# Input stage of a hybrid decoder step: the sample sequences' mLSTM state products on column tiles and row tiles of TensorE

## The reference

```python
m_t = jnp.maximum(inter, jnp.max(dlog, axis=-1))
wts = jnp.exp(dlog - m_t[..., None]) * jnp.einsum('bhtd,bhsd->bhts', q_c, k_c)
w_prev = jnp.exp(inter - m_t)
num = w_prev[..., None] * jnp.einsum('bhtd,bhde->bhte', q_c, C) + jnp.einsum('bhts,bhse->bhte', wts, v_c)
den = w_prev * jnp.einsum('bhtd,bhd->bht', q_c, n) + jnp.sum(wts, axis=-1)
h = num / jnp.maximum(jnp.abs(den), jnp.exp(-m_t))[..., None]
...
C = wp[..., None, None] * C + jnp.einsum('bhs,bhsd,bhse->bhde', ws, k_c, v_c)
```

## Time and profile before

| | |
|---|---|
| median of 3 runs | 1915.89 us (1915.38 to 1916.56) |
| profiled execution, its own time | 1918.07 us |
| its span | 1916.1 us |
| mean granted TensorE clock | 0.96 |
| DMA | 408.98 MB, mean 213 GB/s |

### The profile page before, as it was taken

How to read it: one execution, slowest core, us unless ns; L and a number is a source line. 1 busy time by engine, 2 the same in 40 slices (tenths; PEclk the granted TensorE clock), 3 DMA queues, 4 the chain that set the end, 5 groups by cost and what they waited for, 6 DMA issues and landing times. The chain is left out here.

```text
span 1916.1 us, 36779 instructions
## 1 busy us (share of the span) xinstructions
PE 1748.7 (91%) x14891; PEld 1439.4 (75%) x14891; DVE 910.2 (48%) x1610; ACT 604.8 (32%) x890; POOL 270.5 (14%) x286
## 2 busy tenths in 40 slices
PE   7999999999999999999998999999898868777675
PEld 7999899998787778778777999999796434443242
DVE  6553445555756676576665445455423222121223
ACT  5243223333443344344335333335432101110012
POOL 0550003112010100100010000850050000000002
PEclk9999999999999999999998999999998988898888
DMA  7445353434232223233215446455638999999995
GB/s 270 174 155 187 110 179 117 173 135 167 100 112 90 99 101 122 87 112 112 90 55 204 155 175 250 152 220 214 238 159 338 422 431 432 431 431 431 431 431 248
DMA packets 46600, 408.98 MB, mean 213 GB/s; under 512 B 6580, under 2 KB 8376, under 8 KB 16696
## 3 DMA queue, kind: packets, MB, share of 16 engines
q1 hardware_dynamic: 46520, 407.81, 54.2%
HBM read 396.62 MB, written 11.18 MB: 213 GB/s over the span
## 5 line engine op out<-in xcount | busy, mean ns | idle before, releaser
L387 PE MATMUL ps<-x_high,w_high 128*128 128x288 f32 x928 | 257.4, 303 | 9.3 <-ACT w_high L593 9.3
L388 PE MATMUL ps<-x_rest,w_high 128*128 128x288 f32 x928 | 253.1, 299 | 0.0
L387 PEld LDWEIGHTS ps<-x_high,w_high 128*128 128x128 f32 x928 | 177.1, 191 | 12.8 <-ACT w_high L593 10.2
L388 PEld LDWEIGHTS ps<-x_rest,w_high 128*128 128x128 f32 x928 | 177.1, 191 | 0.5
L549 ACT ACTIVATE w_high<-w_raw 128x2048 fp32r<-128x2048 f32 x57 | 109.2, 1915 | 153.9 <-DMA w_raw<-in_w_main 77.5
L1101 PE MATMUL ps<-x_high,r_high 128*128 128x288 f32 x512 | 145.8, 308 | 3.8 <-ACT r_high L1352 3.8
L660 DVE TENSOR_TENSOR w_rest<-w_raw,w_high 128x2048 fp32r<-128x2048 f32 x58 | 137.1, 2369 | 11.0 <-ACT w_high L549 11.0
L2557 PE MATMUL ps<-half_a,xg 128*32 128x512 f32 x240 | 81.4, 840 | 62.3 <-DMA half_b<-in_w_egu 62.0
L1101 PE MATMUL ps<-rx_low,r_high 128*128 128x288 f32 x480 | 134.7, 305 | 0.0
L392 PE MATMUL ps<-x_high,w_rest 128*128 128x288 f32 x928 | 132.1, 295 | 1.0 <-DVE w_rest L660 1.0
L392 PEld LDWEIGHTS ps<-x_high,w_rest 128*128 128x128 f32 x928 | 126.0, 188 | 1.2 <-DVE w_rest L660 1.2
(11 more groups left out here) (600 smaller groups left out, 3824.1 us busy)
## 6 DMA issues: line engine op xcount, KB each, us to landing
w_raw<-in_w_main SPq DMA_DIRECT2D x57, 1024.0 KB, 4.8
ring<-in_w_g SPq DMA_DIRECT2D x32, 1024.0 KB, 4.8
half_a<-in_w_egu SPq DMA_DIRECT2D x15, 2048.0 KB, 18.0
half_b<-in_w_egu SPq DMA_DIRECT2D x15, 2048.0 KB, 22.3
ring<-in_w_u SPq DMA_DIRECT2D x32, 512.0 KB, 4.2
ring<-in_w_gate SPq DMA_DIRECT2D x8, 2048.0 KB, 7.8
ring<-in_w_out SPq DMA_DIRECT2D x8, 2048.0 KB, 7.8
half_d<-in_w_egu SPq DMA_DIRECT2D x8, 2048.0 KB, 20.7
```

Of the source, the lines that this page charges most:

```text
L387: mm(o, high[:, t % 2, k, :], x_h[:, k, :], start=(k == 0), stop=False)
L388: ins = mm(o, high[:, t % 2, k, :], x_l[:, k, :], start=False, stop=False)
```

## The change

The products of the sample states run four sequences at a time. For the queries, sequence b adds to partitions 32(b mod 4) to 32(b mod 4)+32 of bank 0, a column tile of the array of its own; `cq` then has 128 rows, and the product that adds it to the numerators sums its four quadrants with a 128 x 32 constant (four identities under each other). For the keys, `decode_state` takes the rows of quadrant b mod 4, a row tile of its own, in a bank of its own (4, 5, 1, 3); all eight products stand in one group after the third group of tiles, and VectorE reads both halves of it at the places where it did. For this, the sample tokens of the values, keys and gate rows must stand on all four quadrants: each transpose of 32 columns becomes four products with the identity, one for each quadrant. `ktm` becomes 128 x 256 instead of 32 x 1024. `scores` of the next head now waits for `cB`, since banks 1 and 3 hold states.

```diff
+QUADS = P // NSM
+    c["own_seq"] = ((s % NSM) // NL == s // NSM + (P // NSM) * np.arange(NB // QUADS)[None, :])
...
-        ktm = placed("ktm", [NSM, NB, P], "ring", 14336)
+        ktm = placed("ktm", [P, NB // QUADS, P], "ring", 14336)
-        cq = placed("cq", [NSM, DV], "front", 10272)
+        cq = placed("cq", [P, DV], "front", 10272)
+        quad = lambda n: slice(NSM * n, NSM * n + NSM)
+        state_banks = (4, 5, 1, 3)
...
             def turn_values(e):
                 for c in range(3):
-                    n = P if c < 2 else NSM
                     for j in range(4):
-                        ins = nc.tensor.transpose(ps[0:n, b, j * P:(j + 1) * P], mlu[:, 8 + 4 * e + j, c * P:c * P + n], ident)
+                        o, own = ps[:, b, j * P:(j + 1) * P], mlu[:, 8 + 4 * e + j, :]
+                        if c < 2:
+                            ins = nc.tensor.transpose(o, own[:, c * P:c * P + P], ident)
+                        else:
+                            for n in range(QUADS):
+                                ins = mm(o[quad(n), :], own[:, NPR:T], ident, start=True, stop=True)
             def scores(h):
+                    pe.wait_ge(v.sem, v.at(f"cB{h - 1}"))
...
-                for c in range(3):
-                    n = P if c < 2 else NSM
-                    ins = nc.tensor.transpose(ps[0:n, 7, c * P:(c + 1) * P], kh[:, c * P:c * P + n], ident)
+                for c in range(2):
+                    nc.tensor.transpose(ps[:, 7, c * P:(c + 1) * P], kh[:, c * P:(c + 1) * P], ident)
+                for n in range(QUADS):
+                    ins = mm(ps[quad(n), 7, 2 * P:3 * P], kh[:, NPR:T], ident, start=True, stop=True)
             def numerators(h):
-                if h:
-                    pe.wait_ge(v.sem, v.at(f"cB{h - 1}"))
                 for b in range(NB):
-                    ins = mm(ps[0:NSM, 0, 0:DV], qz[:, NSM * b:NSM * b + NSM], cst[:, h % 2, b, :], start=(b == 0), stop=(b == NB - 1))
+                    ins = mm(ps[quad(b % QUADS), 0, 0:DV], qz[:, NSM * b:NSM * b + NSM], cst[:, h % 2, b, :],
+                             start=(b < QUADS), stop=(b >= NB - QUADS))
...
-                    ins = mm(ps[:, 4 + e, NPR:T], cq[:, e * P:(e + 1) * P], K("ident", NSM)[:, 0:NSM], start=False, stop=True)
+                    ins = mm(ps[:, 4 + e, NPR:T], cq[:, e * P:(e + 1) * P], K("ident_c"), start=False, stop=True)
-            def decode_state(h, part):
-                if part == "A":
-                    pe.wait_ge(g_.sem, g_.at(f"ktm{h}"))
-                    pe.wait_ge(v.sem, v.at(f"h{h}"))
-                else:
-                    pe.wait_ge(v.sem, v.at(f"cA{h}"))
-                for j in range(4):
-                    b = j + 4 * (part == "B")
-                    ins = mm(ps[:, 4 + j // 2, j % 2 * DV:(j % 2 + 1) * DV], ktm[:, b, :], vt[0:NSM, 2, h * DV:(h + 1) * DV],
+            def decode_state(h):
+                pe.wait_ge(g_.sem, g_.at(f"ktm{h}"))
+                pe.wait_ge(v.sem, v.at(f"h{h}"))
+                for b in range(NB):
+                    n, m = b % QUADS, b // QUADS
+                    ins = mm(ps[:, state_banks[n], m * DV:(m + 1) * DV], ktm[quad(n), m, :], vt[quad(n), 2, h * DV:(h + 1) * DV],
                              start=True, stop=True)
...
                 if t == GIF + 9:
-                    for c in range(3):
-                        n = P if c < 2 else NSM
-                        for i, r in enumerate((g, ws)):
-                            ins = nc.tensor.transpose(ps[0:n, 7, c * 8 + 4 * i:c * 8 + 4 * i + 4], r[:, c * P:c * P + n],
-                                                      K("ident", 4, 0, 4))
+                    for i, r in enumerate((g, ws)):
+                        for c in range(2):
+                            nc.tensor.transpose(ps[:, 7, c * 8 + 4 * i:c * 8 + 4 * i + 4], r[:, c * P:(c + 1) * P], K("ident", 4, 0, 4))
+                        for n in range(QUADS):
+                            ins = mm(ps[quad(n), 7, 16 + 4 * i:20 + 4 * i], r[:, NPR:T], K("ident", 4, 0, 4), start=True, stop=True)
...
-                decode_state(h, "A")
+                decode_state(h)
                 if h:
                     mean_square(h - 1)
                 tiles(h, 3)
-                decode_state(h, "B")
```

More of the change, by code:

```diff
@@ L270, in stage_front @@
             at_end = lambda *s: [f"{x}{h}" for x in s] if h == MLH - 1 else []
-            pe_steps += [f"{x}{h}" for x in ("s", "b", "k", "c", "n", "u", "dA")] + of_last("q") + [f"dB{h}"] + at_end("q")
+            pe_steps += [f"{x}{h}" for x in ("s", "b", "k", "c", "n", "u", "d")] + of_last("q") + at_end("q")
             dve_steps += [f"{x}{h}" for x in ("x", "qw", "qn", "w", "wm", "k", "max", "rec", "h", "n", "cA")]
@@ L471, in prompt_state @@
                 q.done(mm(ps[:, 7, DV + 1:DV + 1 + NB], kt[0:NSM, 2, :], K("of_seq", NSM), start=True, stop=True), f"u{h}")
-            def decode_state(h, part):
-                if part == "A":
-                    pe.wait_ge(g_.sem, g_.at(f"ktm{h}"))
-                    pe.wait_ge(v.sem, v.at(f"h{h}"))
-                else:
-                    pe.wait_ge(v.sem, v.at(f"cA{h}"))
-                for j in range(4):
-                    b = j + 4 * (part == "B")
-                    ins = mm(ps[:, 4 + j // 2, j % 2 * DV:(j % 2 + 1) * DV], ktm[:, b, :], vt[0:NSM, 2, h * DV:(h + 1) * DV],
+            def decode_state(h):
[4 more added lines that the diff above has]
+                    ins = mm(ps[:, state_banks[n], m * DV:(m + 1) * DV], ktm[quad(n), m, :], vt[quad(n), 2, h * DV:(h + 1) * DV],
                              start=True, stop=True)
-                q.done(ins, f"d{part}{h}")
+                q.done(ins, f"d{h}")
             def mean_square(h):
@@ L568, in values @@
                 for c in range(3):
-                    n = P if c < 2 else NSM
                     act.wait_ge(q.sem, q.at(f"vt{c}{e}"))
                     b = (0, 1, 3, 4, 5, 7)[3 * e + c]
-                    a.done(fn(vt[0:n, c, e * 512:(e + 1) * 512], ps[0:n, b, :], ACT.Copy), f"vt{c}{e}")
+                    a.done(fn(vt[:, c, e * 512:(e + 1) * 512], ps[:, b, :], ACT.Copy), f"vt{c}{e}")
             def square_of(h):
@@ L607, in _ @@
                     act.wait_ge(q.sem, q.at("gt"))
-                    fn(gt[:, 0:16], ps[:, 7, 0:16], ACT.Copy)
-                    a.done(fn(gt[0:NSM, 16:24], ps[0:NSM, 7, 16:24], ACT.Copy), "gt")
+                    a.done(fn(gt[:, 0:24], ps[:, 7, 0:24], ACT.Copy), "gt")
                 if GIF + 11 <= t < GIF + 15:
@@ L628, in _ @@
                 act.wait_ge(q.sem, q.at(f"c{h}"))
-                a.done(fn(cq[:, :], ps[0:NSM, 0, 0:DV], ACT.Copy), f"c{h}")
+                a.done(fn(cq[:, :], ps[:, 0, 0:DV], ACT.Copy), f"c{h}")
                 act.wait_ge(q.sem, q.at(f"n{h}"))
@@ L740, in weights @@
                 ts(kt[:, 1, :], ps[:, 7, P:2 * P], wsp(1), None, ALU.mult)
-                v.done(ts(kt[0:NSM, 2, :], ps[0:NSM, 7, 2 * P:3 * P], wsp(2, NSM), None, ALU.mult), f"k{h}")
+                v.done(ts(kt[:, 2, :], ps[:, 7, 2 * P:3 * P], wsp(2), None, ALU.mult), f"k{h}")
             def outcome(h):
@@ L764, in state @@
             def state(h, part):
-                dve.wait_ge(q.sem, q.at(f"d{part}{h}"))
-                for j in range(4):
-                    b = j + 4 * (part == "B")
+                dve.wait_ge(q.sem, q.at(f"d{h}"))
+                for j in range(QUADS):
+                    b = j + QUADS * (part == "B")
                     ins = stt(out=cst[:, h % 2, b, :], in0=cst[:, h % 2, b, :], scalar=wps[h % 2][:, NL * b + NL - 1:NL * b + NL],
-                              in1=ps[:, 4 + j // 2, j % 2 * DV:(j % 2 + 1) * DV], op0=ALU.mult, op1=ALU.add)
+                              in1=ps[:, state_banks[j], (b - j) // QUADS * DV:((b - j) // QUADS + 1) * DV], op0=ALU.mult, op1=ALU.add)
                 v.done(ins, f"c{part}{h}")
@@ L887, in by_sequence @@
                 if h:
-                    pool.wait_ge(q.sem, q.at(f"dB{h - 1}"))
-                g_.done(tt(ktm[:, :, :], kt[0:NSM, 2, :].unsqueeze(1).to_broadcast([NSM, NB, P]),
-                           K("of_seq", NSM).unsqueeze(2).to_broadcast([NSM, NB, P]), ALU.mult), f"ktm{h}")
+                    pool.wait_ge(q.sem, q.at(f"d{h - 1}"))
+                g_.done(tt(ktm[:, :, :], kt[:, 2, :].unsqueeze(1).to_broadcast([P, NB // QUADS, P]),
+                           K("own_seq").unsqueeze(2).to_broadcast([P, NB // QUADS, P]), ALU.mult), f"ktm{h}")
             def gated(h):
```

## The result

The median of six runs is 1904.9 us (1902.88 to 1910.31), beside 1916.22 us for the kernel before: ratio 0.9937, 95% interval [0.9923, 0.9951]. The change makes the kernel faster by 11 us; forecast were 19, and the median lies above the range of 1893.5 to 1902.5. The profiled execution has a time of 1902.88 us and a span of 1900.9.

A forecast was written before the change was run, and what follows sets the result against it. The prediction took TensorE (PE) to bound the changed stage, with the last ten slices bound by expert-weight transfers. Terms -10.1 - 10.8 + 2.1 = -18.8, rounded to -19, took the median from 1915.9 to 1897 us; range 1893.5 to 1902.5.

The forecast's parts named there:

- The query products: Changed stage: 16 passes per head on four column tiles take 1.05 us instead of 3.57, gain 10.1 us in all.
- The state products: Changed stage: one group of 1.15 us per head on four row tiles replaces two of 1.92, gain 10.8 us.
- rival 1: State products: row tiles overlap only twofold, so states gain 7.7 us and the time is 1900.2 us; chance 0.12.
- wide weight loads: State group on row tiles: 0.1 us more than the fourfold overlap gives, for 1.15 us.
- Added work: Extra PE passes for keys, value turns and gate rows in the changed stage: 2.1 us in sum (1.8 to 2.8).
- Keys: Each head's key samples: one transpose becomes four products, eight passes; +0.24 us a head, 1.0 us in all.
- First value turn: Four transposes become 16 products, 32 passes, in a full PE stream: +0.5 us.
- Gates: Gate rows: two transposes of six become 16 tiny passes, +0.4 us.
- Waits, cover, clock: Next scores' wait for the state update has 11.1 us of cover, costing nothing; the half-clock stretch stays in the main case.
- Costed at nothing: Items given no cost: query-sum product and copies, GpSimd's masked keys, gate copies; no DMA or queue entry moves.
- Rival 5: No change: the saving is given back in a later wait or at a fixed start among the transfers; chance 0.02.
- my own case's range: The main case, probability 0.79: 1894.5 to 1899.5 us, with 0.5 us of scatter included.

## Why the prediction was wrong

- *The query products*: forecast gain 10.1 us, measured 4 x 2.57 = 10.3.
- *The state products*: forecast 10.8, measured 4 x 2.76 = 11.0. Fourfold, so rival 1 is out, and no extra for wide weight loads.
- *Added work*: mis-sized. Keys 0.72 us a head instead of about 0.30 (265.88 to 266.18 us before): 1.7 us where 1.0 was forecast. First value turn 1.98 instead of 1.23 (183.60 to 184.83): 0.75 for 0.5. Second, from its start to the scores, 2.82 instead of 2.29 (192.01 to 194.30): 0.5 for 0.2, since the last bank's 32 passes took 1.08 us and ScalarE had run out of banks to copy. Gates 0.39 for 0.4; the forecast had read 0.46 us as their cost before, which is the length of the records, where the distance is 0.38. Sum 3.4 instead of 2.1. What I left out: each change between full and tiled passes costs 0.1 us or a little more (an estimate: in the turn of the keys two transposes take 262.50 - 262.14 = 0.36 us where the forecast's prices give 0.21, the eight passes 0.36 where they give 0.23).
- *The stage*: 473.59 - 454.71 = 18.9 us, forecast 19. The terms above give 17.9. About 0.4 us more is the tile behind the removed second state group, whose first product took 0.24 us to the next start where others take 0.13. The rest I can't assign; over all profiles the first product behind the barrier starts between 471.6 and 474.1 us with the old stream on PE and between 453.4 and 455.5 with the new one, so it lies within the scatter, and the 18.9 of this pair is partly luck.
- *Waits, cover, clock*: as forecast; 10.6 us of cover, no new wait, the stretch at half clock stays.
- **The step that failed** is in "Costed at nothing": "No DMA and no queue entry moves", and with it "The last ten slices [...] keep their length". The transfers kept their order and sizes, but the destinations of all behind the constants moved in SBUF by 32 bytes, through two columns of constants that I read as data only. With that placement the last stage's transfers ran at 427 to 429 GB/s instead of 431. Rival 5 asked for "a fixed start among the transfers" and looked at when they start, not at where they land. Shown: the changed kernel with the old addresses has the ratio 0.9896, which is 1896.3 us on the time before, where 1897 was forecast. What the placement takes is 0.3% or 5 us by the ratios 0.9923 and 0.9896 (their intervals overlap a little), 4.4 and 3.5 us by the kernel before moved by 32 and by 64 bytes, and 3.3 us by the lengths to the last landing.
- The rest of the miss is scatter: the same changed kernel came to 0.9937 in the first comparison and 0.9923 in the second, and the time before itself lies between 1914.9 and 1924.8 us over all runs. Of the 7.7 us between forecast and measured gain, 3.8 stand between the two profiled executions (the 4.0 given back in the expert stage above all) and 3.9 come from comparing medians instead of these two. 0.5 us of scatter in my own case's range was far too little.

## What to carry to other kernels

Before an edit is costed at nothing, ask what it does to the addresses of everything allocated behind it. Here 32 to 128 bytes in front of the ring took 0.6 to 0.8% off the rate of a stage bound by transfers; a ring that started at a multiple of 256 bytes never showed the loss. Which tile has to stand there is not settled, so keep the whole row of tiles where it was when one in front of it grows, or move it by a multiple of 256 bytes, and read the rate afterwards. Small f32 products gained fourfold on column tiles and on row tiles alike, whether the tile changed after two or after four passes; each row tile had a bank of its own, and nothing else was run. Budget 0.2 us for a group's entry and exit and 0.1 us for every switch between full and tiled passes. Compare profiled executions with each other and medians with each other: in this kernel the two differ by 2 us either way.

## What the runs showed of the hardware

- Four row tiles of 32 by 128, f32, 256 columns, in four banks: 16 passes in 1.08 us, against 8 in 1.92 us one after the other. Four tiles that write the same partitions, each in its own bank, did not hold each other back.
- Several passes in a row on one tile hold nobody else back: on column tiles 1.02 us with four in a row, 1.00 with two; on row tiles 1.10 and 1.08.
- A ring of landing tiles that starts off a multiple of 256 bytes: 426 to 430 GB/s instead of 430 to 432 in the stage bound by transfers, with rows of 16 KB that take 614.8 to 615.5 ns in the mean instead of 611. In the rate, 128 bytes off is nearly as bad as 32 (428.4 and 427.6 GB/s in the mean of the slices).
- The address of the written row does not decide alone: rows at the same two off-boundary places take 611 ns while the ring stands at its multiple of 256, and are as slow as all others when it doesn't.
